# Two transformer blocks on one core: the first block's modulation as row dots beside the projections, norms beside the opening products, constants and gate rows made early

## The chip, the core and the metric

The kernel runs on one core of a Trainium2 chip. A core has TensorE (PE, matrix products into PSUM; the profile shows its weight loads as PEld), VectorE (DVE), ScalarE (ACT), GpSimd (POOL) and SyncE (SP, which here issues nearly all DMA transfers). The engines run side by side and wait for each other on semaphores. The metric is device time in microseconds, the median of the runs.

## The reference

Sequence 256, width 1024, everything in fp32. The first block takes `x` and a context `ctx` of 256 tokens; the second block has four layers. What the change touches of the first:

```python
mod_l = jax.nn.silu(c) @ ada_w[i] + ada_b[i]          # 6 x 1024 columns
mod_c = jax.nn.silu(c_ctx) @ ada_w[i] + ada_b[i]
hl = rmsnorm(xl, norm1_g[i]) * (1.0 + sc1) + sh1      # and hc from the context
yc, yl = token_mixing(hc, hl, w_in[i], w_out[i], ...) # recurrence, neighbour attention, short convolution
xl = xl + g1 * yl
hl2 = rmsnorm(xl, norm2_g[i]) * (1.0 + sc2) + sh2
xl = xl + g2 * peer_ffn(hl2, ...)                     # 16 of 16384 experts in each of 8 heads
return rmsnorm(xl, final_g)
```

In the second block each layer computes `mod = silu(c) @ ada_w[i] + ada_b[i]` with 9 x 1024 columns, and runs a feed-forward part, a mixer (a sparse attention with compressed keys, stick-breaking, differential, sparse again) and a second feed-forward part, each behind a norm that is scaled and shifted by `mod`.

## The kernel before

The program is a series of blocks. In a block each engine has its own instruction list; between two blocks all five engines meet. So an operation that stands alone in a block holds everybody.

Weights of the projections come as items of 1 MB through a ring of six slots (`issue_w`), weights of the modulation as items through a ring of four slots (`issue_a`, `a_ring`). SP issues an item when its slot has been used. A unit is sixteen products of 128x256, two halves with eight steps of the contraction each; the profile shows an fp32 product as two instructions.

The first block, in order:
- An input block loads seven tensors; ACT makes the Silu of both conditions (L3169 on).
- `ada_stage`: DVE adds `item * cond[k]` into two accumulators of 128x2048, for eight items and two conditions. The partition sum is still open.
- `mod1_columns_stage`: `mod_columns` closes it on PE, one product with a column of ones for every 128 columns of the accumulator, so 32 products with one moving column (L377).
- `norm_stage`, twice, for `x` and for the context: squares on ACT, root, scaling on DVE, 16 transposes on PE, gain and shift on ACT into `hT` and `hcT`.
- `first_projections`: 21 units on PE with `hT` and `hcT`. Beside them the side work of `loads` and `work`: SP issues up to four modulation items behind each weight item, DVE multiplies and adds them (L238) into `rest` and `acc`. These are the other 4 x 1024 columns of the first block's modulation and the 9 x 1024 of the second block's layer 0.
- `mod1_rest_stage`: 104 products with the column of ones, then bias, gain and shift.
- `neighbour_stage`: loads the relative bias of the eight heads (2 MB), masks it on POOL with four selects, makes the short convolution on DVE, then runs the attention.
- `recurrent_mixer`: loads seven constants and waits for them, then four tile stages, `rw_chain_stage` (two chains of eight states, forward and backward, a link each for PE and DVE in turn) and `rw_output_stage`, which loads `g_up`.
- `rows1_stage`: spreads four modulation rows over all partitions, 32 products with the identity (L2567). Then output projection, second norm, and `peer_stage`, in which POOL gathers the experts' rows and DVE and PE weigh them.
- `final_norm_stage` loads `final_g` and `mod_stage` spreads three gate rows (24 products, L409).

In the second block, `compress` loads two constants and waits; `diff_stage` has a block of its own between projections and attention, which loads two constants and makes one scalar of them; `second_block` opens with two tables that ACT loads and waits for.

The order of each engine's list is the order in which the functions are called; no planner moves anything.

Of the kernel before, what the change touches and what calls it, by code (L numbers as in the profile page):

```python
# [39 lines left out]
M_COLS = 2 * D  # L40
MIXERS = ("nsa", "stick", "diff", "nsa")
# [55 lines left out]
class Core:  # L97


    def __init__(self, nc, ctx):  # L100
        self.nc = nc
        self.ctx = ctx
        self.signals = {}
        self.serial = 0
# [14 lines left out]
    def semaphore_of(self, name):  # L119
        if name not in self.signals:  # L120
            self.signals[name] = Signal(self.ctx.enter_context(self.nc.semaphore(name)))
        return self.signals[name]

    def sb(self, ctx, name, shape, dtype=F32):
        self.serial += 1
        return ctx.enter_context(self.nc.sbuf_tensor(f"{name}_{self.serial}", shape, dtype))
# [74 lines left out]
    def issue_a(self, sp, take):  # L201

        for n in range(self.a_issued, self.a_issued + take):
            if n >= self.a_first + A_SLOTS:
                sp.wait_ge(self.a_used, n - A_SLOTS + 1)
            if n < MOD1_ITEMS:
                sp.dma_start(self.a_ring[:, n % A_SLOTS, 0:M_COLS], self.m_stream[n]).then_inc(
                    self.a_loaded[n % A_SLOTS], 16)
            else:
                sp.dma_start(self.a_ring[:, n % A_SLOTS, :], self.a_stream[n - MOD1_ITEMS]).then_inc(  # L210
                    self.a_loaded[n % A_SLOTS], 16)
# [10 lines left out]
    def load_a(self, sp, n, turn=0):  # L222

        sp.wait_ge(self.a_used, turn * A_SLOTS + (n - A_SLOTS + 1))
        src = self.a_stream[bass.ds(turn * A_SLOTS + (n - MOD1_ITEMS), 1), :, :]
# [3 lines left out]
    def mod_unit(self, dve, n, cond, acc, turn=0, opens=False):  # L229
# [4 lines left out]
        if opens:  # L234
            last = dve.tensor_scalar(acc, item, cond, None, ALU.mult)
        else:
            dve.wait_ge(self.a_used, turn * A_SLOTS + (n - 1))
            last = dve.scalar_tensor_tensor(out=acc, in0=item, scalar=cond, in1=acc, op0=ALU.mult, op1=ALU.add)  # L238
# [24 lines left out]
def norm_stage(core, post, pre, of=None):  # L263

    nc = core.nc
    squares, roots = core.semaphore_of("squares_ready"), core.semaphore_of("roots_ready")
    means, rows = core.semaphore_of("means_ready"), core.semaphore_of("rows_ready")
    turned, x_new = core.semaphore_of("turned_ready"), core.semaphore_of("x_new")  # L270

    x, hT, gain, shift = of or (core.x, None, core.gain, core.shift)
    whole_made = core.semaphore_of("h_whole_made")
    y = core.y
    n_post = 1 if post is not None else 0
    n_pre = 1 if pre is not None else 0
    with ExitStack() as ctx:
        junk = core.sb(ctx, "junk", [P, 2, D])
        ss = core.sb(ctx, "ss", [P, 2, 2 * TT])
        stat = core.sb(ctx, "stat", [P, 4, TT])  # L280
        xn = core.sb(ctx, "xn", [P, TT, D])

        whole = junk[:].rearrange("p t (k n) -> p (t k) n", n=T)
        block = ctx.enter_context(nc.Block())

        @block.sync
        def _(sp):
            core.issue_w(sp, 0)

        @block.scalar  # L290
        def _(act):
            if n_post:
                for i in range(2 * TT):

                    act.activation(junk[:, i // 2, (i % 2) * BANK:(i % 2 + 1) * BANK], y[:, i, :], ACT.Square,
                                   accum_out=ss[:, 0, i:i + 1]).then_inc(squares.sem, 1)
                act.wait_ge(means.sem, means.at(1))
                act.activation(stat[:, 0, :], stat[:, 0, :], ACT.Sqrt).then_inc(roots.sem, 1)
# [1697 lines left out]

# [1381 lines left out]
```

## Time and profile before

| | us |
|---|---|
| median of 3 runs | 3866.25 (3865.90 to 3875.92) |
| the profiled execution, its time / span | 3875.92 / 3875.5 |
| PE busy | 3151.6 (81% of the span) |
| DVE busy | 2452.2 (63%) |
| ACT busy | 1294.1 (33%) |
| POOL busy | 569.5 (15%) |
| DMA moved | 860.09 MB, mean 222 GB/s |

The shares are means over stages with different limits. An engine that is idle says something only together with what the others do in the same stretch, and PE's granted clock (1.00 is 2.4 GHz, 0.50 is 1.2 GHz) has to be read beside PE's busy time.

### The profile page before, as it was taken

How to read it: one execution, taken by the hardware profiler on the slowest of the kernel's cores; microseconds unless marked ns; L12 is line 12 of the kernel's file. 1: busy time of each engine (PE TensorE's matmuls, PEld its weight loads, DVE VectorE, ACT ScalarE, POOL GpSimd, SP SyncE). 2: the span in 40 equal slices, each digit the busy share in tenths (PEclk: the TensorE clock that was granted, in tenths of full speed). 3: DMA queues.
4: the chain of work that ended last, by engine and by line, in shares of the span. 5: the costliest groups of instructions: out<-in, count | busy, mean ns of one | idle time of the engine just before them, and what ended most of it. 6: DMA issues, size and time to landing. Idle time of an engine off the chain costs nothing. (4 is left out here: it accounts for less than half of the span.)

```text
span 3875.5 us, 53219 instructions
## 1 busy us (share of the span) xinstructions
PE 3151.6 (81%) x21732; PEld 2669.1 (69%) x21732; DVE 2452.2 (63%) x3818; ACT 1294.1 (33%) x2068; POOL 569.5 (15%) x310
## 2 busy tenths in 40 slices
PE   3965776566665659988999998899998899997899
PEld 3854665322221129987898996898997799987798
DVE  3654553788888867736586854686853686543654
ACT  1003321111111123436434345434344434342733
POOL 0001001344444520030000013000004000012000
PEclk9966787777766679987999997999998999996999
DMA  4971001899999968631585842484943484553143
GB/s 184 403 304 44 2 3 57 307 368 375 382 369 390 391 285 353 228 145 44 218 323 209 355 146 97 194 340 190 367 155 124 190 344 152 185 184 121 45 175 129
DMA packets 118255, 860.09 MB, mean 222 GB/s; under 512 B 15152, under 2 KB 16304, under 8 KB 17712
## 3 DMA queue, kind: packets, MB, share of 16 engines
q1 hardware_dynamic: 80912, 588.77, 39.4%
q0 software_dynamic: 36864, 268.45, 17.3%
q8 instruction: 127, 2.08, 0.2%
q14 instruction: 64, 0.52, 0.0%
q10 hardware_dynamic: 288, 0.26, 0.0%
HBM read 856.38 MB, written 1.05 MB: 221 GB/s over the span
## 5 line engine op out<-in xcount | busy, mean ns | idle before, releaser
L252 PE MATMUL ps<-h_hi,w_hi 128*128 128x256 f32 x3328 | 951.7, 286 | 38.4 <-DVE h_lo L533 16.0
L254 PE MATMUL ps<-h_hi,w_lo 128*128 128x256 f32 x3328 | 947.4, 285 | 0.0
L253 PE MATMUL ps<-h_lo,w_hi 128*128 128x256 f32 x3328 | 947.4, 285 | 0.0
L179 DVE TENSOR_TENSOR w_lo<-w_ring,w_hi 128x2048 fp32r<-128x2048 f32 x284 | 649.7, 2290 | 466.4 <-ACT w_hi L174 464.8
L174 ACT ACTIVATE w_hi<-w_ring 128x2048 fp32r<-128x2048 f32 x330 | 630.0, 1914 | 683.1 <-PE ps L254 556.6
L252 PEld LDWEIGHTS ps<-h_hi,w_hi 128*128 128x128 f32 x3328 | 640.7, 193 | 52.1 <-issue 22.0
L253 PEld LDWEIGHTS ps<-h_lo,w_hi 128*128 128x128 f32 x3328 | 640.5, 192 | 3.2
L254 PEld LDWEIGHTS ps<-h_hi,w_lo 128*128 128x128 f32 x3328 | 640.5, 192 | 0.0
L2958 PE MATMUL ps<-expert_rows,expert_diag 128*128 128x512 f32 x512 | 381.0, 889 | 290.3 <-ACT expert_diag L2996 290.1
L179 POOL TENSOR_TENSOR w_lo<-w_ring,w_hi 128x2048 fp32r<-128x2048 f32 x46 | 212.2, 4632 | 2276.4 <-ACT w_hi L174 2276.4
L2958 PEld LDWEIGHTS ps<-expert_rows,expert_diag 128*128 128x128 f32 x512 | 120.7, 259 | 544.6 <-ACT expert_diag L2996 442.6
L2920 POOL DMA_INDIRECT expert_rows<-in_experts,expert_idx x256 | 343.9, 1343 | 415.5 <-DVE expert_sum L3108 218.1
L238 DVE SCALAR_TENSOR_TENSOR mod_acc<-a_ring,cond,mod_acc 128x2304 f32<-128x2304 f32 (+1 forms) x138 | 353.6, 2588 | 52.9 <-DMA a_ring<-in_a_stream 25.4
L3094 DVE CUSTOM_DVE_ANT_0 expert_junk<-expert_rows,h 128x1024 f32<-128x1024 f32 x256 | 309.6, 1224 | 102.4 <-DMA expert_rows<-in_experts,expert_idx 102.2
L254 PE MATMUL ps<-w_hi,hid_lo 128*128 128x512 f32 x704 | 277.2, 394 | 0.0
L252 PE MATMUL ps<-w_hi,hid_hi 128*128 128x512 f32 x704 | 275.4, 391 | 0.0
L253 PE MATMUL ps<-w_lo,hid_hi 128*128 128x512 f32 x704 | 275.3, 391 | 0.0
L2981 ACT ACTIVATE expert_coef<-expert_dot 128x2 f32<-128x2 f32 x128 | 26.0, 203 | 488.6 <-DVE expert_dot L3094 488.5
L252 PE MATMUL ps<-w_hi,h_hi 128*128 128x256 f32 x544 | 159.5, 293 | 19.1 <-POOL w_lo L179 9.7
L3108 DVE SCALAR_TENSOR_TENSOR expert_sum<-expert_rows,expert_coef,expert_sum 128x1024 f32<-128x1024 f32 x128 | 164.5, 1285 | 4.5
L253 PE MATMUL ps<-w_lo,h_hi 128*128 128x256 f32 x544 | 158.2, 291 | 0.0
L254 PE MATMUL ps<-w_hi,h_lo 128*128 128x256 f32 x544 | 158.2, 291 | 0.0
(454 smaller groups left out, 4319.7 us busy)
## 6 DMA issues: line engine op xcount, KB each, us to landing
w_ring<-in_w_stream SPq DMA_DIRECT2D x360, 1024.0 KB, 4.9
a_ring<-in_a_stream SPq DMA_DIRECT2D x128, 1152.0 KB, 11.0
a_ring<-in_m_stream SPq DMA_DIRECT2D x24, 1024.0 KB, 9.7
mod_acc<-in_mod_start SPq DMA_DIRECT2D x6, 2304.0 KB, 8.8
alibi<-in_alibi SPq DMA_DIRECT2D x3, 2048.0 KB, 8.7
expert_rows<-in_experts,expert_idx POOLq DMA_INDIRECT x256, 9.2
a_ring<-in_norm_post_row SPq DMA_DIRECT2D x3, 1024.0 KB, 4.7
na_bias<-in_na_bias SPq DMA_DIRECT2D x1, 2048.0 KB, 8.0
```

What stands on the lines that cost most here:

```text
L174: act.activation(self.w_halves(n)[0], self.w_item(n), ACT.Copy).then_inc(self.hi_made, 1)
L179: pool.tensor_tensor(self.w_halves(n)[1], self.w_item(n), self.w_halves(n)[0], ALU.subtract).then_inc(self.lo_made, 1)
L238: last = dve.scalar_tensor_tensor(out=acc, in0=item, scalar=cond, in1=acc, op0=ALU.mult, op1=ALU.add)
L252: pe.matmul(out, stationary[0], moving[0], start=start, stop=False)
L253: pe.matmul(out, stationary[0], moving[1], start=False, stop=False)
L254: return pe.matmul(out, stationary[1], moving[0], start=False, stop=stop)
L2920: pool.indirect_dma_start(rows[:, slot, :], None, core.io["experts"], bass.IndirectOffsetOnAxis(ap=idx[:, n // UNIT, at:at + 1], axis=0)). ...
L2958: last = pe.matmul(core.y[:, 2 * t + half, :], diag[:, b % G_BATCHES, :], rows[:, n % G_SLOTS, D + half * BANK:D + (half + 1) * BANK], sta ...
L2981: act.activation(coef[:, b % G_BATCHES, :], dot[:, b % G_BATCHES, :], ACT.Gelu_apprx_tanh).then_inc(acts.sem, 1)
L3094: last = dve.tensor_tensor_reduce(junk[:, e, :], rows[:, slot, 0:D], core.h2[:, tile_of(n), :], 1.0, 0.0, ALU.mult, ALU.add, dot[:, b % G_ ...
L3108: dve.scalar_tensor_tensor(out=acc[:, t, :], in0=rows[:, n % G_SLOTS, D:2 * D], scalar=c[:, 0:1], in1=acc[:, t, :], op0=ALU.mult, op1=ALU. ...
```

## The change

1. **Opening.** `opening_stage` replaces five blocks. PE multiplies the conditions, as two stationary columns, with the items themselves, so that the sum over the partitions comes at once: 8 items x 4 banks, products of 2x512. The norms of `x` and the context run on DVE beside them, and PE's 32 transposes of them stand between the products of items 3 and 4 and between those of 6 and 7. Two rows of 2048 come out; 16 small transposes turn them into columns.
2. **Row dots.** The other modulation weights come transposed, 52 items of 1 MB with two groups of 128 output columns each. An output column's weights lie along a partition, so one `tensor_tensor_reduce` with the condition row gives the finished column (`mod_dots`); its elementwise output goes back into the item. `mod1_rest_stage` is gone.
3. **Constants early.** The neighbours' bias goes out first in the projections' block and POOL masks it there; the convolution moves to POOL beside the attention (`beside`); the recurrence's constants and `g_up` are loaded in the opening, `final_g` in `peer_stage`, the compression's and the differential attention's in the projections ahead. ACT's wait for two tables moves to DVE in the attention (`prepare`), and so does the scalar of the differential attention.
4. **Wide rows.** `rows1_stage` and `mod_stage` are gone; their 14 half rows are made inside `rw_chain_stage`, one behind each link (`widen`), with ACT's copies.
5. In the expert loop the dot's elementwise output goes back into the gathered row, and DVE no longer waits there for its own previous dots.

```diff
+    def mod_dots(self, dve, n, cond_row, cols):
+        dve.wait_ge(self.a_loaded[n % A_SLOTS], (n // A_SLOTS + 1) * 16)
+        for b in range(2):
+            rows = self.a_ring[:, n % A_SLOTS, b * D:(b + 1) * D]
+            last = dve.tensor_tensor_reduce(rows, rows, cond_row, 1.0, 0.0, ALU.mult, ALU.add, cols[:, b:b + 1])
+        last.then_inc(self.a_used, 1)
...
+        @block.tensor            # opening_stage
+            pe.wait_ge(cond_made.sem, cond_made.at(1))
+            for k in range(KD):
+                pe.wait_ge(core.a_loaded[k % A_SLOTS], (k // A_SLOTS + 1) * 16)
+                for c in range(M_COLS // BANK):
+                    last = pe.matmul(core.ps[0:2, c, :], cond[:, k, :],
+                                     core.a_ring[:, k % A_SLOTS, c * BANK:(c + 1) * BANK],
+                                     start=(k == 0), stop=(k == KD - 1))
+                last.then_inc(core.a_used, 1)
+                if k == 3:
+                    pe.wait_ge(ident_in.sem, ident_in.at(16))
+                    turns(0, xn)
+                if k == 6:
+                    turns(1, xc)
+            pe.wait_ge(rows_out.sem, rows_out.at(2))
+            for c in range(2 * KD):
+                last = pe.transpose(core.ps[:, 0, 2 * c:2 * c + 2], rows[:, c * P:(c + 1) * P], core.ident[0:2, 0:2])
...
+            def loads(sp, items):
+                sp.dma_start(a.na_bias[:], core.io["na_bias"]).then_inc(bias_in.sem, 16)
+                total = core.a_taken + T_ITEMS
+                for _ in range(items):
+                    core.issue_w(sp, 1)
+                    core.issue_a(sp, min(-(-T_ITEMS // items), total - core.a_taken))
...
+            def widen(i):        # rw_chain_stage
+                cols = halves[i][0]
+                if i >= 4:
+                    pe.wait_ge(wide_kept.sem, wide_kept.at(i - 3))
+                for j in range(4):
+                    last = pe.matmul(core.y[:, i % 4, j * P:(j + 1) * P], wide(cols[:, j], P), core.ident[:],
+                                     start=True, stop=True)
+                last.then_inc(wide_out.sem, 1)
...
-                if b:
-                    dve.wait_ge(dots.sem, dots.at(b))
...
-                    last = dve.tensor_tensor_reduce(junk[:, e, :], rows[:, slot, 0:D], ...
+                    last = dve.tensor_tensor_reduce(rows[:, slot, 0:D], rows[:, slot, 0:D], ...
```

Three places show how the lists change. PE's list in the opening, before (`mod_acc` are DVE's sums, `xn` the scaled tokens):

```order
L377 MATMUL ps<-ones,mod_acc 128x1 x32
L2485 UNCONDITIONAL_BRANCH
L353 UNCONDITIONAL_BRANCH [waits barrier_Pool_Activation_PE_DVE_SP_release]
L359 MATMUL ps<-identity,xn 128x128 [waits rows_ready]
L359 MATMUL ps<-identity,xn 128x128 x15
L277 UNCONDITIONAL_BRANCH
L353 UNCONDITIONAL_BRANCH [waits barrier_Pool_Activation_PE_DVE_SP_release]
L359 MATMUL ps<-identity,xn 128x128 [waits rows_ready]
L359 MATMUL ps<-identity,xn 128x128 x15
L277 UNCONDITIONAL_BRANCH
```

and after (`cond` are the two stationary columns; the tile `na_bias` lends its room to the scaled tokens and `na_v` to the two rows):

```order
L2465 MATMUL ps<-a_ring,cond_42 2x512 [waits a_loaded3]
L2465 MATMUL ps<-a_ring,cond_42 2x512 x3
L2456 MATMUL ps<-identity,na_bias 128x128 [waits open_scaled,ident_in]
L2456 MATMUL ps<-identity,na_bias 128x128 x15
L2465 MATMUL ps<-a_ring,cond_42 2x512 [waits a_loaded0]
L2465 MATMUL ps<-a_ring,cond_42 2x512 x3
L2465 MATMUL ps<-a_ring,cond_42 2x512 [waits a_loaded1]
L2465 MATMUL ps<-a_ring,cond_42 2x512 x3
L2465 MATMUL ps<-a_ring,cond_42 2x512 [waits a_loaded2]
L2465 MATMUL ps<-a_ring,cond_42 2x512 x3
L2456 MATMUL ps<-identity,na_bias 128x128 [waits open_kept,open_scaled]
L2456 MATMUL ps<-identity,na_bias 128x128 x3
```

The products follow the items one by one, and the norms' transposes stand among them; the five meetings of the engines in the first list are one. DVE's list beside the projections, before and after:

```order
L238 SCALAR_TENSOR_TENSOR mod_acc<-a_ring,cond_25,mod_acc 128x2048 [waits a_used,a_loaded2]
L238 SCALAR_TENSOR_TENSOR mod_acc<-a_ring,cond_25,mod_acc 128x2048 [waits a_used,a_loaded3]
L238 SCALAR_TENSOR_TENSOR mod_acc<-a_ring,cond_25,mod_acc 128x2048 [waits a_used,a_loaded0]
L238 SCALAR_TENSOR_TENSOR mod_acc<-a_ring,cond_25,mod_acc 128x2048 [waits a_used,a_loaded1]
L238 SCALAR_TENSOR_TENSOR mod_acc<-a_ring,cond_25,mod_acc 128x2048 [waits a_used,a_loaded2]
```

```order
L252 ISA a_ring,mod_cols_38<-a_ring,cond_rows 128x1024 [waits a_loaded0]
L252 ISA mod_cols_38 128x1
L252 ISA a_ring,mod_cols_38<-a_ring,cond_rows 128x1024
L252 ISA mod_cols_38 128x1
L252 ISA a_ring,mod_cols_38<-a_ring,cond_rows 128x1024 [waits a_loaded1]
```

A scalar multiply and add over 2048 or 2304 columns becomes two reductions of 1024, each followed by the read of its accumulator; the wait for the item before last (`a_used`) is gone. PE's list in the chain of states, before and after:

```order
L2349 MATMUL ps<-state,psi 64x64 x3
L2349 MATMUL ps<-state,psi 64x64 [waits state_kept1]
L2349 MATMUL ps<-state,psi 64x64 x3
L2349 MATMUL ps<-state,psi 64x64 [waits state_kept0]
L2349 MATMUL ps<-state,psi 64x64 x3
L2349 MATMUL ps<-state,psi 64x64 [waits state_kept1]
```

```order
L2225 MATMUL ps<-state,psi 64x64 x3
L2217 MATMUL ps<-identity,cols_15 128x128 [waits mod_wide_kept]
L2217 MATMUL ps<-identity,cols_15 128x128 x3
L2225 MATMUL ps<-state,psi 64x64 [waits state_kept1]
L2225 MATMUL ps<-state,psi 64x64 x3
L2217 MATMUL ps<-identity,cols_15 128x128 [waits mod_wide_kept]
L2217 MATMUL ps<-identity,cols_15 128x128 x3
L2225 MATMUL ps<-state,psi 64x64 [waits state_kept0]
```

Behind the four products of each link stand four wide ones, from the fifth group on with a wait for ACT's copy of four groups before.

## Rows read from the trace of the kernel before

**Rows 1.** Stretch, us; busy PE, PEld, DVE, ACT, POOL; PEclk, DMA share, GB/s.
```profile
93.30:264.00 170.70, 134.65 (x624) 118.56 (x622) 114.49 (x48) 12.33 (x21) 0.00 (x0) 0.90 0.98 406
228.00:264.00 36.00, 0.00 (x0) 0.00 (x0) 29.02 (x12) 0.58 (x1) 0.00 (x0) 0.54 0.99 414
264.20:309.00 44.80, 44.50 (x208) 44.45 (x208) 0.39 (x2) 0.00 (x0) 0.00 (x0) 0.50 0.01 3
695.00:1415.00 720.00, 424.13 (x718) 158.56 (x717) 595.80 (x1262) 92.14 (x285) 343.92 (x256) 0.73 0.94 377
1452.30:3875.50 2423.20, 2245.98 (x15856) 2082.61 (x15856) 1480.09 (x1958) 1056.91 (x1513) 193.91 (x42) 0.93 0.52 200
```

**Rows 2.** Timeline, opening and first projections: start, us, engine, operation.
```profile
17.79 31.76 DVE L917 SCALAR_TENSOR_TENSOR mod_acc<-a_ring,cond,mod_acc 128x2048 f32<-128x2048 f32 x14
...
80.59 3.75 ACT L308 ACTIVATE hcT<-ps,shift,gain 128x256 f32<-128x256 f32 x8 [2.86 <-PE ps L359]
...
84.63 8.63 PE L977 MATMUL ps<-w_ring,hT 128*128 128x256 f32 x32 [1.52 <-PEq L277]
106.92 7.07 PE L977 MATMUL ps<-w_ring,hcT 128*128 128x256 f32 x32
```

**Rows 3.** Stretches with 128x512 fp32 products alone, at either clock.
```profile
714.00:718.00 4.00, 3.78 (x4) 1.17 (x4) 4.00 (x11) 0.36 (x2) 1.68 (x1) 0.50 1.01 426
1409.10:1412.90 3.80, 3.70 (x8) 1.44 (x8) 2.23 (x4) 0.40 (x2) 0.00 (x0) 1.00 1.00 414
```

**Rows 4.** DMA issues of the first 100 us: size, median us to landing.
```profile
x<-in_x_in SPq DMA_DIRECT2D x1, 1024.0 KB, 4.9
```

**Rows 5.** Stretches with small PE instructions: the chain of states, the wide rows.
```profile
574.60:590.00 15.40, 14.61 (x134) 13.31 (x135) 12.52 (x30) 0.00 (x0) 0.00 (x0) 0.54 0.01 2
610.00:615.10 5.10, 5.05 (x46) 4.86 (x44) 1.52 (x4) 1.79 (x3) 0.00 (x0) 1.00 0.00 0
```

**Rows 6.** Page, part 5: two groups of one shape on ACT and POOL.
```profile
L174 ACT ACTIVATE w_hi<-w_ring 128x2048 fp32r<-128x2048 f32 x330 | 630.0, 1914 | 683.1 <-PE ps L254 556.6
L179 POOL TENSOR_TENSOR w_lo<-w_ring,w_hi 128x2048 fp32r<-128x2048 f32 x46 | 212.2, 4632 | 2276.4 <-ACT w_hi L174 2276.4
```

**Rows 7.** Timeline of DVE: last modulation item, and a reduction of 1024.
```profile
261.29 2.62 DVE L238 SCALAR_TENSOR_TENSOR mod_acc<-a_ring,cond,mod_acc 128x2304 f32<-128x2304 f32 x1 [0.18 <-DMA a_ring<-in_a_stream]
...
1418.53 1.23 DVE L3318 CUSTOM_DVE_ANT_0 final_junk<-x 128x1024 f32<-128x1024 f32 x1
```

**Rows 8.** Timeline around the neighbour attention: before it, its start, after it.
```profile
309.83 0.17 DVE L2548 SCALAR_TENSOR_TENSOR cols<-mod_sums,norm_g 128x8 f32<-128x8 f32 x1
...
334.82 2.08 PE L2641 MATMUL ps<-na_kT,na_qT 64*128 64x512 f32 x4 [26.09 <-PEq L2701]
...
378.65 0.42 DVE L2116 TENSOR_TENSOR kk<-k,rw_rows 128x256 f32<-128x256 f32 x1 [9.76 <-PEq L2752]
```

**Rows 9.** The masks' stretch, and DVE's 128x256 operation in and out of it.
```profile
318.00:332.50 14.50, 0.00 (x0) 0.00 (x0) 13.73 (x7) 0.00 (x0) 13.25 (x4) 0.50 0.00 0
...
322.36 11.44 DVE L2737 SCALAR_TENSOR_TENSOR sc_o<-sc_u,sc_w,sc_o 128x256 f32<-128x256 f32 x6
...
387.82 0.42 DVE L2132 SCALAR_TENSOR_TENSOR early<-early,rw_rows 128x256 f32<-128x256 f32 x1
```

**Rows 10.** Timeline: wide rows, final gain, gate rows, first products of two stages.
```profile
605.65 9.41 PE L2567 MATMUL ps<-identity,cols 128*128 128x128 f32 x64 [0.93 <-PEq L2394]
...
1426.86 2.48 DVE L3325 SCALAR_TENSOR_TENSOR x<-x,final_ss,final_g 128x1024 f32<-128x1024 f32 x2 [6.45 <-DMA final_g<-in_final_g]
...
1429.64 6.96 PE L409 MATMUL ps<-identity,gate_cols 128*128 128x128 f32 x48 [16.79 <-PEq L3299]
...
1440.90 7.17 PE L543 MATMUL ps<-ones_r 128*128 128x512 f32 x20 [4.30 <-PEq L1841]
...
2964.10 2.53 PE L1465 MATMUL ps<-kT,qT 64*128 64x128 f32 x12 [7.18 <-PEq L1759]
```

**Rows 11.** Tile cmp_blk: its engine sat idle until, us, times.
```profile
  DMA cmp_w<-in_cmp_w: 9.2, 2
```

More of the change, by code:

```diff
@@ L374, in mod_columns @@
-def mod_columns(core, pe, acc, chunks, bank):
-    for c in range(chunks):
-        last = pe.matmul(core.ps[:, bank, c:c + 1], acc[:, c * P:(c + 1) * P], core.ones[:, 0:1],
-                         start=True, stop=True)
-    return last
 def shape_columns(core, dve, layer, cols, subs):
@@ L1007, in _ @@
         def _(pool):
+            if side:
+                side[2](pool)
             for n in splits:
@@ L2333, in rw_chain_stage @@
     y_done = core.semaphore_of("rw_y_done")
+    wide_out, wide_kept = core.semaphore_of("mod_wide"), core.semaphore_of("mod_wide_kept")
+    wide_rows = [(m.cols[:, v, :], m.rows[:, v, :]) for v in range(4)]
+    wide_rows += [(core.gate_cols[:, sub, :], core.gates[:, sub, :]) for sub in range(3)]
+    halves = [(cols[:, 4 * half:4 * half + 4], row[:, half * BANK:(half + 1) * BANK])
+              for cols, row in wide_rows for half in range(2)]
     def part(d):
@@ L2468 @@
 PROJ1 = 14
-MOD1_FIRST = KD
 class Mod1:
@@ new lines, in constants @@
+            def constants(sp):
+                io = core.io
+                for dst, src in ((g[:], io["norm2_g"]), (core.norm_pre[:], io["norm_pre"]),
+                                 (core.norm_post[:], io["norm_post"]),
+                                 (bias[:, 0:REST_COLS], io["mod_bias1"][:, 2 * KD:]),
+                                 (bias[:, REST_COLS:], io["mod_bias2"][:, 0, 0, :])):
+                    sp.dma_start(dst, src).then_inc(late_consts.sem, 16)
+                sp.dma_start(a.sc_w[:], io["sc_w"]).then_inc(conv_in.sem, 16)
+                tables.load(core, sp)
@@ new lines, in work @@
+            def work(dve):
+                done = core.dve_steps.done
+                for i in range(T_ITEMS):
+                    row = cond_row[:, 0 if 2 * i < REST_COLS else 1, :]
+                    core.mod_dots(dve, MOD1_FIRST + i, row, cols[:, 2 * i:2 * i + 2])
+                dve.wait_ge(late_consts.sem, late_consts.at(80))
+                dve.wait_ge(core.a_used, A_BASE)
+                done(dve, dve.tensor_tensor(cols[:], cols[:], bias[:], ALU.add))
+                rest = cols[:, 0:REST_COLS].rearrange("p (v k) -> p v k", v=4)
+                by_sub = cols[:, REST_COLS:].rearrange("p (s a k) -> p s a k", s=3, a=3)
+                shape_columns(core, dve, 0, by_sub, range(3))
+                dve.tensor_tensor(core.gate_cols[:], by_sub[:, :, 2, :], core.norm_post[:], ALU.mult)
+                done(dve, dve.tensor_copy(m.cols[:], rest))
+                dve.scalar_tensor_tensor(out=m.cols[:, 2, :], in0=rest[:, 2, :], scalar=1.0, in1=g[:],
+                                         op0=ALU.add, op1=ALU.mult)
@@ L3227, in first_block @@
             short.close()
-            recurrent_mixer(core, a, outT)
-        m.rows = core.sb(ctx, "rows1", [P, 4, D])
-        rows1_stage(core, m)
+            m.rows = core.sb(ctx, "rows1", [P, 4, D], side="right")
+            recurrent_mixer(core, m, a, tables, outT)
         with ExitStack() as s0:
```

703 lines of the change are left out of this document (278 added, 425 removed).

## The prediction

> **What bounds the kernel now.** I read the busy time by stretches first, then the timeline of each stretch in which TensorE (PE) is idle, then the waits on DMA in the later stages. The stretches show four kinds of bound. From 93.3 to 264.0 us the DMA share is 0.98 at 406 GB/s: the weights of the projections and of the modulation go through one pipe, and in the last 36 us of it (228 to 264) PE does nothing at all while the DMA share is 0.99. From 264.2 to 309 us PE does 208 LDWEIGHTS-bound instructions with one moving column each, all others idle. From 695 to 1415 us the gather of the experts holds the DMA engines at 0.94. From 1452 to the end PE is busy 2246 of 2423 us at a clock of 0.93; no line of that work changes, apart from three waits [rows 1]. So the change can gain only in the serial places around these.
>
> The opening is serial: VectorE (DVE) sums eight items for two conditions until 49.55 us (17.79 + 31.76), PE adds up the columns, the two norms follow one after the other, and the projections begin at 84.63 us [rows 2].
>
> **Part 1, the opening.** Added: 32 products of 2 x 512 (eight items, four banks). An fp32 product shows as two instructions, so 64. A 128x512 instruction of the same kind took 3.78/4 = 0.945 us at clock 0.50 and 3.70/8 = 0.46 us at 1.00 [rows 3]; they have 128 stationary columns where the new ones have 2, but the moving 512 columns set the time. The input x landed 4.9 us after its issue [rows 4]; x is now issued at about 1.2 us and the first item right behind it, at 1 MB in 2.5 us (406 GB/s), so item 0 is there at about 8.6 us. PE starts at the low clock. At 84.63 us the first 32 instructions of the projections took 8.63 us where 32 later ones took 7.07 [rows 2], an excess of 1.6 us, so some 3.3 us at the low level; I take 4 of the 64 instructions at 0.945 us and 60 at 0.46 = 31.5 us. The 32 transposes of the norms lie between them on PE: 46 instructions of that width took 5.05 us at clock 1.00, 0.11 each [rows 5], so 3.5 us. PE is done at 8.6 + 31.5 + 3.5 = 43.6 us. DMA isn't the limit: ten pieces of 2.5 us land by about 29 us when the ring is free, and each item takes PE 3.7 us. The norm's squares and scaling on DVE (about 5 us each) end before PE reaches them. Behind PE's last product: a copy of 2 x 1024 (1.1 us and a hop of 0.25), 16 transposes of two rows (0.11 to 0.23 each, I take 1.8 us), DVE's sums, shift and gain (0.9), ACT's eight pieces (3.75, [rows 2]), a table load and the two Silu, the wide one of the shape that takes ACT 1.91 us [rows 6], with the load 3.4 us together, and 0.3 us to the next stage (84.34 to 84.63 in [rows 2]). Sum 55.1 us, against 84.6: **gain 29.5**. Bounds: all 64 at the low clock is 64 x 0.945 = 60.5 us in place of 31.5, gain 0.5; with all at 0.46 it is gain 31.5.
>
> **Part 2, dots beside the projections.** The side work was 16 items of 1 MB and 32 of 1.125 MB, 52 MB; it is now 52 items of 1 MB, again 52 MB. The stretch stays bound by DMA where it was (0.98 of 170.7 us, [rows 1]), so it keeps its length: 179.3 us from PE's start to the last sum (84.6 to 263.9). DVE per item: two dots of 1024. Such a reduction took 1.23 us [rows 7], so with the hop 2.5 us for 1 MB, against 2.62 us for 1.125 MB. That is 52 x 2.5 = 131 us of 179: not the bound, though inside a burst of four items it is level with DMA's 2.5 us. The 2 MB of the neighbours' bias go out ahead of the rest, in the 8.7 us in which the queue waits for PE's first unit anyway: 0. The dots end at 55.1 + 179.3 = 234.4 us. I bound this by -3 (a shorter last item) and +8.
>
> **Part 3, what followed them.** Gone: the 208 column sums, the load of the bias and its masks, the convolution on DVE. Between the last item (261.29 + 2.62 = 263.91, [rows 7]) and the first score product (334.82, [rows 8]) lay 70.9 us. What is left of it on DVE is a dozen operations of 0.17 us in a chain (row of 309.83, [rows 8]), 1.2 us, and the change of stage, 0.3: **gain 69.4**. The masks now run on GpSimd (POOL) beside the first dots, the convolution on POOL beside the attention: four two-input operations of 512 at 4632/2048 = 2.26 ns a column [rows 6] are 4.6 us, six of 256 some 3.5, with memset and waits 10 us, below the 34 us of that stage (334.82 to 378.65 less 9.76, [rows 8]). Hidden, but not free: while POOL's masks ran, DVE's 128x256 operation took 11.44/6 = 1.9 us and without them 0.42 [rows 9], 4.5 times as long. Beside the attention this can touch ten microseconds of DVE work of which one operation in a dozen is of that kind: between 0 and +8, I take **-3**. Beside the dots, masks (13.3 us [rows 9] from the landing of the bias at about 8 us after PE's start) and dots (from 16 us after it) overlap some 6 us: DVE loses 4.5 us and has 3.3 us of slack in each of the first bursts, which come two units of 6.9 us apart (7.07 with its overlap, [rows 2]): 0 in the sum, +4.5 as the bound.
> The Trainium skill, page GPSIMD Engine Reference, section 8 Key points, says that GpSimd shares its SBUF interfaces with VectorE and that Vector instructions with two SBUF inputs contend; every dot is one. By that rule the trace's factor holds for the dots too, and the sum is up to 4.5 us smaller.
>
> **Part 4, smaller waits.** The recurrence's constants come early: its first DVE operation sat idle 9.76 us [rows 8]; left are ACT's tanh and the change of stage, 0.65: **gain 9.1**. The rows of the second modulation: PE 9.41 us plus 0.93 us of edge go [rows 10], and 14 groups of four products (112 instructions) go into the chain of states. That chain takes some 15 us for seven pairs of links, 2.1 us each, on PE at clock 0.54, 134 instructions in 14.6 us or 0.11 each [rows 5]. The new instructions cost 112 x 0.11 = 12 us at the full clock and twice that at the low one. A pair of links then holds twice eight link instructions (0.44 us at the full clock) and twice eight new ones (0.88), 2.6 us instead of 2.1: +3.8 for seven pairs, +2 until the clock rises, and -2 for the 64 output instructions behind it, which find the clock up; PE becomes the engine that is late: +4. At the low clock (0.88 + 1.76) x 2 = 5.3 us per pair: +22. DVE waits for the link products, and nobody but PE's own queue stands behind a group; ACT's 14 copies of 512 columns, some 0.5 us each by the rate of [rows 6], fit. **Gain 10.3 - 4 = 6.3**, down to -12. The later gate rows go whole: 6.96 us and an edge of 1.0: **8.0**. The final gain row: DVE's 6.45 us wait, **6.4**. ACT's wait for two tables is inside PE's 4.30 us gap at 1440.9; its issues stay: **2.0**, between 0 and 4. The compression's constants: **9.2** in two waits [rows 11]. The differential attention's separate stage: PE idle 7.18 us, of which the issue-free rest is kept: **5.2** [rows 10]. The dropped wait in the expert loop and the in-place output gain 0, since the gather holds that stage at 0.94 of DMA [rows 1]; one broadcast of 0.5 MB ahead of it costs at most 1.3 us, which I leave in the range.
>
> **The sum.** 29.5 + 69.4 - 3 + 9.1 + 6.3 + 8.0 + 6.4 + 2.0 + 9.2 + 5.2 = 142.1 us. The profiled execution took 3875.92 us, so it would take 3733.8; the median of the runs is 9.7 us below it, so 3866.25 - 142.1 = **3724 us**.
>
> **The rivals.**
> *The opening stays at the low clock.* The granted clock stayed at 0.50 through 44.8 us in which PE was busy 44.5 of them with one-column products [rows 1], and at 0.54 in the chain of 64x64 ones [rows 5]: being busy isn't enough. For the rise: 128x512 instructions did run at 1.00 [rows 3], and the new ones stream as many columns. Time 3724 + 29 = 3753.
> *The chain of states stays at the low clock.* 3724 + 18 = 3742. For it: 0.54 there now; against it: the same products as a block got 1.00 from 610 us on [rows 5].
> *POOL slows DVE more than the slack covers.* At the upper bounds, 4.5 + (8 - 3) = 9.5: 3734.
> *The dots become the bound, slower than before.* If a dot in place took much longer than 1.26 us, the stretch would be 52 items long on DVE. Place: the projections. It overtakes DMA from 179.3/52 = 3.4 us per item, and eats the whole gain at (170.7 + 142)/52 = 6.0 us per item, 3.0 us per dot; at 3.3 us per dot the kernel would take 3866 + 31 = 3897. Against it: the in-place sum of 2304 columns took 2.62 us, 1.14 ns a column [rows 7], and the reduction out of place takes 1.23 for 1024, 1.20 ns; only POOL's factor of 4.5 would reach it, and POOL works 13 of those 171 us.
> *Nothing is won,* because the stage is bound by DMA alone: against it, DMA idles in nearly all of the removed places.
>
> **How the numbers follow.** Forecast 0.62 (own range 3710 to 3738); opening at the low clock 0.17; chain at the low clock 0.12; POOL 0.06; dots the bound 0.02; nothing won 0.01. The range reaches down to the better bounds (-18: clock, last item, waits) and up to the first rival: 3706 to 3756. This kernel's measurement tells 0.3%, 12 us, from no change. Faster 0.97, same 0.01, slower 0.02.
>
> **What would show it.** Projections begin at about 55 us (84 if the first rival holds), with PE's granted clock 1.00 over most of 12 to 43 us. First neighbour scores at about 236 us. From there to the recurrence's first DVE operation 35 to 37 us, without the 9.8 us gap. The chain of states 19 to 20 us long. From 264 us on no one-column products. The forecast is wrong if the dots take over 1.7 us each, if PE waits for items in the opening, or if the clock of the second block isn't within 0.01 of 0.93.

## The result, and the profile after

The changed kernel takes 3762.20 us (median of 4 runs, 3761.18 to 3767.77), the kernel before 3871.09 us (4 runs, three of them those under "Time and profile before"; 3865.90 to 3883.90). The ratio is 0.9715, 95% interval 0.9696 to 0.9734: faster. The forecast was 3724 us, range 3706 to 3756. The direction was right, the size wasn't: the change was to save 142 us, and the two spans differ by 3875.5 - 3760.8 = 114.7 us.

Long stretches of the kernel after (stretch, us; busy PE, PEld, DVE, ACT, POOL; PEclk, DMA share, GB/s). They answer to [rows 1] and, in the chain of states, to [rows 5]:

```profile
12.00:43.00 31.00, 31.00 (x93) 8.39 (x91) 4.13 (x8) 2.15 (x5) 0.00 (x0) 1.00 0.99 387
...
62.50:236.40 173.90, 135.25 (x627) 118.72 (x625) 127.83 (x208) 12.33 (x21) 13.29 (x4) 0.90 0.98 399
...
473.50:515.40 41.90, 41.87 (x224) 37.13 (x224) 12.21 (x29) 7.76 (x13) 0.00 (x0) 0.51 0.00 1
515.40:520.00 4.60, 4.52 (x65) 4.33 (x64) 0.69 (x1) 0.60 (x1) 0.00 (x0) 0.50 0.00 0
585.20:1326.20 741.00, 444.03 (x832) 177.47 (x832) 610.39 (x1328) 94.45 (x288) 341.61 (x256) 0.74 0.93 371
1347.00:3760.80 2413.80, 2248.99 (x15856) 2084.97 (x15856) 1480.67 (x1958) 1056.73 (x1513) 193.94 (x42) 0.93 0.53 201
```

From 12 to 43 us the opening shows a granted clock of 1.00, DMA bounds the projections as before, and the second block has its 0.93. The third row is the surprise: in the chain of states PE is busy 41.87 of 41.90 us, at 0.51, the low one of its two levels (1.2 GHz).

The timeline after, first PE and DVE from the opening to the neighbour attention (start, us, engine, operation), for [rows 2, 7 and 8]:

```profile
9.12 16.17 PE L2465 MATMUL ps<-a_ring,cond 128*2 128x512 f32 x32 [9.12 <-DMA a_ring<-in_m_stream]
...
27.12 10.46 PE L2465 MATMUL ps<-a_ring,cond 128*2 128x512 f32 x24
...
39.41 3.59 PE L2465 MATMUL ps<-a_ring,cond 128*2 128x512 f32 x8
...
53.79 9.28 PE L802 MATMUL ps<-w_ring,hT 128*128 128x256 f32 x32 [8.34 <-PEq L2365]
...
73.04 4.25 DVE L252 CUSTOM_DVE_ANT_0 a_ring<-a_ring,cond_rows 128x1024 f32<-128x1024 f32 x1
...
235.11 1.22 DVE L252 CUSTOM_DVE_ANT_0 a_ring<-a_ring,cond_rows 128x1024 f32<-128x1024 f32 x1
...
237.98 2.93 PE L2561 MATMUL ps<-na_kT,na_qT 64*128 64x512 f32 x6 [40.23 <-PEq L768]
...
274.20 0.42 DVE L1972 TENSOR_TENSOR kk<-k,rw_rows 128x256 f32<-128x256 f32 x1 [0.55 <-PEq L2642]
```

and then the chain of states, the norm, and the first products of the second block and of the differential attention, for [rows 10]:

```profile
475.80 1.11 PE L2225 MATMUL ps<-state,psi 64*64 64x64 f32 x8
...
476.84 2.07 PE L2217 MATMUL ps<-identity,cols 128*128 128x128 f32 x8
...
1331.21 2.48 DVE L3198 SCALAR_TENSOR_TENSOR x<-x,final_ss,final_g 128x1024 f32<-128x1024 f32 x2
1335.59 7.50 PE L399 MATMUL ps<-ones_r 128*128 128x512 f32 x20 [11.97 <-PEq L1680]
...
2847.13 0.93 PE L1326 MATMUL ps<-kT,qT 64*128 64x128 f32 x8 [1.71 <-PEq L768]
```

The wait for `final_g` is gone, the differential attention's 7.18 us are 1.71. A link with its wide group takes 1.04 + 2.00 = 3.04 us (from 475.80 to 476.84, and to the next link at 478.84), and there are fourteen.

Lining both timelines up at the same operations says where the time went. The prediction's terms stand in the last column; a negative gain is time lost.

| from, to | before, us | after, us | gain | forecast |
|---|---|---|---|---|
| start to first projection | 84.63 | 53.79 | 30.8 | 29.5 |
| to the end of the last modulation sum | 179.3 | 182.5 | -3.3 | 0 |
| to the first neighbour score | 70.9 | 1.7 | 69.3 | 69.4 |
| to the recurrence's first DVE operation | 43.8 | 36.2 | 7.6 | 6.1 |
| four tile stages | 196.4 | 199.3 | -2.9 | 0 |
| chain, outputs, rows, to the output projection's first product | 49.7 | 67.6 | **-17.9** | **+6.3** |
| output projection, norm, to the expert stage | 44.5 | 44.0 | 0.5 | 0 |
| expert stage, to the last update of x | 746.3 | 741.0 | 5.2 | 0 |
| to the second block's first product | 25.4 | 9.4 | 16.1 | 16.4 |
| second block | 2434.6 | 2425.2 | 9.4 | 14.4 |

Up to the recurrence 104.4 us are gained where 105.0 were forecast. One line alone is far off, by 24.2 us.

### The profile page after: what moved, and what is told of

Read it like the earlier page. It is cut to its first block and busy times, and to the rows that moved or that the text cites. A ratio compares the mean times of both kernels' runs of the same rounds, so it can differ in the third digit from the quotient of the medians.

```text
span 3760.8 us, 52720 instructions
## 1 busy us (share of the span) xinstructions
PE 3137.1 (83%) x21540; PEld 2628.7 (70%) x21540; DVE 2418.7 (64%) x3961; ACT 1296.3 (34%) x2066; POOL 580.9 (15%) x321
## 3 DMA queue, kind: packets, MB, share of 16 engines
q0 software_dynamic: 36864, 268.45, 17.9%
q8 instruction: 125, 2.05, 0.2%
## 5 line engine op out<-in xcount | busy, mean ns | idle before, releaser
L266 PE MATMUL ps<-h_hi,w_hi 128*128 128x256 f32 x3328 | 951.0, 286 | 39.5 <-DVE h_lo L389 16.1
L2971 DVE CUSTOM_DVE_ANT_0 expert_rows<-expert_rows,h 128x1024 f32<-128x1024 f32 x256 | 309.1, 1223 | 100.7 <-DMA expert_rows<-in_experts,expert_idx 100.6
L244 DVE SCALAR_TENSOR_TENSOR mod_acc<-a_ring,cond,mod_acc 128x2304 f32<-128x2304 f32 x96 | 247.3, 2613 | 14.6 <-issue 14.1
L252 DVE CUSTOM_DVE_ANT_0 a_ring<-a_ring,cond_rows 128x1024 f32<-128x1024 f32 x104 | 127.5, 1264 | 58.6 <-DMA a_ring<-in_t_stream 55.1
```

The source lines that it names most:

```text
L252: last = dve.tensor_tensor_reduce(rows, rows, cond_row, 1.0, 0.0, ALU.mult, ALU.add, cols[:, b:b + 1])
L266: pe.matmul(out, stationary[0], moving[0], start=start, stop=False)
L2971: last = dve.tensor_tensor_reduce(rows[:, slot, 0:D], rows[:, slot, 0:D], core.h2[:, tile_of(n), :], 1.0, 0.0, ALU.mult, ALU.add, dot[:, b ...
```

## The experiments

**No wide products, or all behind, ahead, or hidden.** The theory: the wide products are paid at the low clock in the chain because of what they stand among. The rivals: they cost that anywhere here, or the chain waits for something else.

wide_none takes the groups out, and ScalarE copies its rows from `x`, so the wide rows are left out of the computation:

```diff
-                    widen(2 * (n - 1) + d)
...
-                act.wait_ge(wide_out.sem, wide_out.at(i + 1))
-                act.activation(row, core.y[:, i % 4, :], ACT.Copy).then_inc(wide_kept.sem, 1)
+                act.activation(row, core.x[:, 0, 0:BANK], ACT.Copy).then_inc(wide_kept.sem, 1)
```

wide_behind puts them behind the last link, wide_ahead the same loop ahead of the first:

```diff
-                    widen(2 * (n - 1) + d)
+            for i in range(len(halves)):
+                widen(i)
```

wide_gaps makes them in three later stages (`make` is `widen` with the bank as an argument):

```diff
+            w.make(pe, 0, core.y[:, 0, :])
             pe.wait_ge(gate.sem, gate.at(1))
...
+            for i in (1, 2):
+                w.make(pe, i, core.y[:, i, :])
             pe.wait_ge(done.sem, done.at(1))
...
+                for i in range(3, 7):
+                    w.make(pe, i, core.ps[:, i - 3, :])
...
+            for i in range(7, 14):
+                m.wide.make(pe, i, core.ps[:, i % 4, :], i - 3 if i > 10 else 0)
             pe.wait_ge(rows.sem, rows.at(TT))
```

> The changed kernel without the 56 wide products in the chain of states (112 instructions): ScalarE fills the four modulation rows and the three gate rows from x instead, so the modulation rows and gates are left out of the computation. Theory A (the wide products hold the chain at TensorE's low clock and PE is what is late): the 14 links shrink from 41.9 us to the 13.8 us that they took in the kernel before (575.05 to 588.89), the rest stays: 3762 - 28 = 3734 us. Rival B (the chain waits for something else too, ScalarE's copies or the semaphores of the groups): the links take clearly more than 14 us, say 20, and the time is 3740 or more. Second question: with no other change the second block's length may still differ by some us from 2425.2, as its clock rises at other moments.

> The same 14 wide groups, but as one block behind the last link, ahead of the output products. Theory A (it is the 64x64 link products between them that keep the clock at 0.50; a block of 128x128 products raises it): links 13.8 us, block 9.41 us for 64 instructions as in the kernel before plus 48 more at 0.11 = 14.7 us, outputs at the full clock 2.3 us: 30.8 us in place of 41.9 + 4.5 = 46.4, so 3762 - 15.6 = 3746 us, with the granted clock at 1.00 in the last ten us of the block. Rival B (the wide products cost 0.26 us each wherever they stand in this stage): 13.8 + 29 + 4.5 = 47.3 us, time 3763 us and a clock of 0.50.

> The same 14 wide groups as one block ahead of the first link, at the start of the chain's stage. Theory A: the block takes 14.7 us with the clock rising in it; the links then start at the full clock and keep it as long as their 64x64 products allow. If the clock stays up, the links take 10 to 11 us instead of 13.8 and the outputs 2.3: 27.5 us in place of 46.4, time 3743 us; if it falls back within the first links, 13.5 + 4.5 us: 32.7 us, time 3748 us. Rival B (0.26 us per wide instruction wherever they stand here): 3763 us.

> The same wide groups moved into places where TensorE idles behind the chain: one ahead of the output gates' products and two behind them (gaps of 3.1 and 5.4 us), four at the head of the output projection (gap of 9.5 us, PE waits for the split weights), seven beside the gated sum and norm (gap of 13.4 us). Theory A: 28.1 us go from the chain; even at 2.07 us a group the first seven fit their gaps, the last seven (14.5 us at the low clock, 7.3 us at the full one) overrun by 1 us at most: 3762 - 28 + 1 = 3735 us. Rival C (what is hidden on PE comes back on ScalarE: its copies stand ahead of the splits and of the root): the output projection or the norm starts 3 to 6 us later, 3740 us. Rival D (PE busy in the gaps has the clock up when the projection starts): 5 us less, 3730 us.

Measured, with the kernel before at 3878.43 us in this batch (9 runs): wide_none 3732.14 us (ratio 0.9625, 0.9611 to 0.9639), wide_behind 3745.82 (0.9658, 0.9643 to 0.9673), wide_ahead 3744.27 (0.9662, 0.9645 to 0.9679), wide_gaps 3732.80 (0.9626, 0.9609 to 0.9642).

The timeline of PE with the block behind the links:

```profile
485.19 9.30 PE L2217 MATMUL ps<-identity,cols 128*128 128x128 f32 x64
494.32 5.52 PE L2217 MATMUL ps<-identity,gate_cols 128*128 128x128 f32 x48
499.78 2.69 PE L2235 MATMUL ps<-state,rw_qT 64*64 64x64 f32 x64
```

The stretches of the kernel with the block ahead: the block's beginning and end, then the links:

```profile
472.50:476.90 4.40, 4.34 (x26) 4.37 (x27) 0.84 (x2) 1.19 (x2) 0.00 (x0) 0.65 0.00 0
477.00:486.80 9.80, 9.80 (x88) 9.74 (x86) 0.00 (x0) 6.47 (x11) 0.00 (x0) 0.99 0.01 2
486.80:489.00 2.20, 1.53 (x26) 1.33 (x24) 1.33 (x4) 0.60 (x1) 0.00 (x0) 1.00 0.00 0
489.00:491.00 2.00, 1.52 (x19) 1.10 (x17) 1.87 (x5) 0.00 (x0) 0.00 (x0) 0.97 0.00 0
491.00:493.00 2.00, 1.77 (x16) 1.78 (x16) 1.60 (x5) 0.00 (x0) 0.00 (x0) 0.50 0.00 0
```

The rival of a fixed price is out: as a block the 112 instructions take 14.6 us in place of 28, and the last 48 take 5.52 us, 0.115 each, less than half of the 0.26 in the chain. Behind the block the outputs take 2.69 us instead of 4.52. Ahead of the links the block has the clock at 1.00, and the links alone lose it again: it is at 0.50 some 4 us after their start. Without wide products the links took 13.5 us, as in the kernel before: nothing else hung on them. Nor is it the chance of one execution: in the five other traces whose chain has the groups in this form (again, expert_wait, no_masks, no_bias and late_consts, all below) it took 41.9 to 42.3 us, at 0.51 each time. Hidden in pauses of PE they cost nothing that shows (3732.80 against 3732.14 without any): wide_gaps already beats both kernels.

**Each group twice.** I had by then a strict form of the theory: the 64x64 products between the groups hold the clock down.

```diff
-                for j in range(4):
+                for j in (0, 1, 2, 3, 0, 1, 2, 3):
```

> The changed kernel with each wide group in the chain made twice (sixteen instructions of 128x128 behind each link's eight of 64x64, in place of eight; the result is the same). Theory A in its strict form (the link products between the groups hold the clock at 0.50 whatever the share of the wide ones): 14 x 2.07 = 29 us more, 71 us for the chain, time 3791 us. Rival L (it is the share of wide products that counts, and 16 to 8 is enough for the clock to rise): the chain ends at 14 x (0.6 + 2 x 1.04) = 38 us with the clock at 1.00, less than the 41.9 us of the single groups, time 3758 us.

Measured: 3761.54 us (4 runs; the kernel before 3879.20; ratio 0.9690, 0.9674 to 0.9707). That time can't be told from the changed kernel's; the trace can. The timeline of PE and the stretch of the chain:

```profile
470.36 3.51 PE L2217 MATMUL ps<-identity,cols 128*128 128x128 f32 x16
473.80 0.80 PE L2225 MATMUL ps<-state,psi 64*64 64x64 f32 x8
474.53 2.05 PE L2217 MATMUL ps<-identity,cols 128*128 128x128 f32 x16
476.51 0.67 PE L2225 MATMUL ps<-state,psi 64*64 64x64 f32 x8
```
```profile
469.70:507.50 37.80, 37.75 (x336) 35.05 (x336) 12.21 (x29) 7.76 (x13) 0.00 (x0) 0.95 0.00 1
```

The strict form falls: with twice the wide products the chain is 4.1 us shorter, sixteen wide instructions take 2.05 us where eight took 2.07, and the clock is 0.95 in the mean. PE was busy all the time in both kernels. So here the clock didn't go by PE's busy time as the profile counts it; with more wide work between the same links it was higher. What it goes by these runs don't tell.

**The groups in the tile stages' pauses.** In the kernels so far the first half of a recurrence tile ran mostly at 0.50, with pauses of 2.64, 3.93 and 1.78 us on PE.

```diff
+WIDE_IN_TILE = ((0, 1, 2, 3), (4, 5, 6, 7), (8, 9, 10), (11, 12, 13))
+            made(pe, own[0])
             for d in range(2):
                 pe.wait_ge(s["wa_out"].sem, s["wa_out"].at(d + 1))
...
+            for i in own[1:-1]:
+                made(pe, i)
             pe.wait_ge(s["p_ready"].sem, s["p_ready"].at(2))
...
+            pe.wait_ge(s["turn1_out"].sem, s["turn1_out"].at(n_ch))
+            made(pe, own[-1])
```

> The changed kernel with its 14 wide groups taken out of the chain of states and set into PE's pauses in the four tile stages ahead of it (4, 4, 3, 3 groups: ahead of the decay sums' products, a pause of 2.64 us; ahead of the transposes, 3.93 us, one or two; behind the triangles, 1.78 us). All are hidden if they take no more than 2.07 us each; 28.1 us go from the chain as in the runs with no or hidden groups. Theory M (the wide products in the pauses raise the clock in the first half of a tile, in which PE now does some 15 us of work at 0.50): up to 5 us a tile less, 3762 - 28 - 20 = 3714 us. Rival N (the clock stays at 0.50 there, and the groups overrun their pauses by about 1 us a tile): 3762 - 28 + 4 = 3738 us.

> The same with each wide group in the tile stages made twice (16 instructions instead of 8; same result). Theory M: the clock rises earlier than with single groups, and a double group then takes 2.05 us, within its pause: as fast as the single groups or faster, 3710 us. Rival N: at 0.50 a double group takes 3.5 us, and the three or four pauses of a tile (2.64, 3.93 and 1.78 us) are overrun by 5 to 6 us: 3734 + 22 = 3756 us.

Measured, with the kernel before at 3878.19 us: wide_tiles 3729.21 us (5 runs, 3723.21 to 3734.46; ratio 0.9620, 0.9601 to 0.9638), wide_tiles2 3721.34 us (5 runs, 3718.96 to 3730.32; ratio 0.9600, 0.9584 to 0.9616). The second tile, 4 to 16 us from its start, in wide_gaps (no groups in the tiles), wide_tiles and wide_tiles2:

```profile
325.90:329.90 4.00, 4.00 (x21) 3.13 (x21) 0.12 (x1) 2.47 (x6) 0.00 (x0) 0.50 0.00 0
329.90:333.90 4.00, 1.71 (x4) 0.80 (x3) 3.42 (x9) 1.10 (x4) 0.00 (x0) 0.50 0.00 2
333.90:337.90 4.00, 2.37 (x11) 2.40 (x12) 1.39 (x4) 0.99 (x2) 0.00 (x0) 0.50 0.00 0
```
```profile
321.30:325.30 4.00, 4.00 (x25) 3.23 (x24) 0.81 (x3) 3.01 (x7) 0.00 (x0) 0.73 0.00 0
325.30:329.30 4.00, 2.51 (x17) 2.31 (x15) 3.76 (x10) 2.30 (x6) 0.00 (x0) 0.84 0.01 2
329.30:333.30 4.00, 2.91 (x24) 2.54 (x28) 0.26 (x1) 1.79 (x3) 0.00 (x0) 0.58 0.00 0
```
```profile
321.20:325.20 4.00, 4.00 (x34) 3.48 (x33) 0.82 (x3) 3.87 (x9) 0.00 (x0) 1.00 0.02 4
325.20:329.20 4.00, 2.67 (x24) 2.48 (x23) 3.76 (x10) 1.43 (x5) 0.00 (x0) 1.00 0.01 2
329.20:333.20 4.00, 2.82 (x78) 2.54 (x79) 0.30 (x2) 1.57 (x3) 0.00 (x0) 1.00 0.00 0
```

Theory M holds in kind: the four tiles take 192.5 and 189.3 us, against 196.4 to 199.9 in the kernels without groups there, so 4 to 7 and 7 to 11 us less in place of the 20 expected. Over the first 24 us of a tile the mean granted clock was 0.50 to 0.64 in the kernel before and the changed one, 0.60 to 0.79 in wide_tiles and 0.86 to 1.00 in wide_tiles2. So the doubled groups, which only repeat a result, had the clock up more, and wide_tiles2 has the lowest median of this study. That it is faster than wide_tiles isn't shown: the 8 us lie within the intervals, and its tiles' 3.2 us rest on one trace each, where kernels with the same tile code differ by 3.5 us.

**The expert stage and the size of chance.** The table shows 5.2 us in the expert stage that I hadn't forecast.

expert_wait is the changed kernel with the wait back; before_inplace is the kernel before with part 5 alone, that is without the wait and with the output in place; again is the changed kernel itself.

```diff
+                if b:
+                    dve.wait_ge(dots.sem, dots.at(b))
```
```diff
-                if b:
-                    dve.wait_ge(dots.sem, dots.at(b))
...
-                    last = dve.tensor_tensor_reduce(junk[:, e, :], rows[:, slot, 0:D], ...
+                    last = dve.tensor_tensor_reduce(rows[:, slot, 0:D], rows[:, slot, 0:D], ...
```

> The changed kernel itself once more, unchanged: a second profiled execution and more times, to see how far stages of the same code differ between executions. So far the expert stage (first query product to the last update of x) took 739 to 745 us in five kernels that have the same code there, and the second block 2421 to 2430 us. Theory E (these are differences between executions): here too it takes some value in 739 to 746 and 2420 to 2431, with no tie to the one seen before (741.1 and 2425.2). Rival F (they are set by the kernel, by when it reaches the stage): within 1 us of 741.1 and 2425.2. Time 3762 us, or up to 3770 in a batch in which the kernel before takes 3878.

> The kernel before with part 5 of the change alone: the dot's elementwise output goes back into the gathered row and VectorE doesn't wait for its previous dots. The expert stage was 746.3 us in the kernel before and 741.1 in the changed one, 5.2 us that my sum didn't have. Theory E (the stage is bound by the gather and differs between executions): a ratio of 1.000 to the kernel before, stage anywhere in 739 to 747 us. Rival G (the edit is worth 5 us): ratio 0.9987, stage 741.

> The changed kernel with the wait for the previous dots put back in the expert loop (the output stays in the gathered row). Theory E: same time as the changed kernel, 3762 us, stage in 739 to 746. Rival G in its other form (it is the wait that cost 5 us before): stage 746 us or more, 3767 us.

Measured, with the kernel before at 3876.50 us (16 runs): again 3760.97 us (0.9705, 0.9684 to 0.9726), before_inplace 3880.04 us (12 runs; 1.0009, 1.0000 to 1.0019), expert_wait 3762.64 us (0.9698, 0.9677 to 0.9720). Their expert stages took 738.6, 741.9 and 742.9 us. Part 5 of the change is worth nothing that these runs resolve, as forecast. Over all traces the expert stage lay between 734.4 and 748.1 us, the changed second block between 2420.6 and 2430.6. The stage in wide_tiles2, one of the longest, and in late_consts (below), the shortest:

```profile
544.40:1291.50 747.10, 442.57 (x832) 178.65 (x832) 610.34 (x1328) 94.45 (x288) 340.02 (x256) 0.75 0.93 368
```
```profile
593.10:1327.40 734.30, 439.14 (x832) 175.15 (x832) 610.72 (x1328) 94.44 (x288) 337.75 (x256) 0.74 0.94 374
```

The same instructions, DVE's busy time within 0.4 us, 368 against 374 GB/s (late_consts has one load of 0.5 MB less there). Terms of 5 us in these two stages can't be read from one trace of each kernel.

**The projections' 3.3 us.** Beside the selects the first two dots take 2.57 and 4.25 us instead of 1.22. Is that loss what lengthens the stretch?

no_masks leaves out the selects, no_bias the load as well:

```diff
-                mask_neighbours(core, pool, a.na_bias, bias_in)
+                pool.wait_ge(bias_in.sem, bias_in.at(16))
```
```diff
-                sp.dma_start(a.na_bias[:], core.io["na_bias"]).then_inc(bias_in.sem, 16)
+                sp.dma_start(a.na_bias[:, 0, 0, 0:16], core.io["na_bias"][:, 0, 0, 0:16]).then_inc(bias_in.sem, 16)
...
+                pool.memset(a.na_bias[:], 0.0)
```

> The changed kernel without the four selects that mask the neighbours' bias (so the mask is left out of the computation; the load of the bias stays). In the changed kernel the dots beside the selects took 2.57 to 4.25 us instead of 1.22, and from PE's first projection to the last dot it took 182.6 us where 179.3 were forecast. Theory H (VectorE's loss beside POOL's selects is what makes the stretch longer): without them 179.3 us, 3.3 us less, 3759 us. Rival I (the stretch is bound by DMA, and the 3.3 us are the 2 MB of the bias ahead of the other items, 5 us at 406 GB/s less some slack): the dots all take 1.22 us, the stretch stays at 182.6 us and the time at 3762 us.

> The changed kernel without the load of the neighbours' bias and without its mask: 8 KB are loaded in place of 2 MB, and POOL fills the tile with zeros (bias and mask are left out of the computation). Theory I (the 2 MB ahead of the first items lengthen the DMA-bound stretch): from PE's first projection to the last dot 179.3 us or less in place of 182.6, down to 177.6 if all 5 us of the load go; time 3762 - 4 = 3758 us. Rival K (the stretch is longer for its first bursts or its smaller items, not for the bias): 182 us again.

Measured: no_masks 3767.13 us (4 runs; ratio 0.9721, 0.9702 to 0.9741), no_bias 3763.06 us (4 runs; ratio 0.9694, 0.9676 to 0.9711); neither time can be told from the changed kernel's. All dots of no_masks, minimum, median and maximum in ns:

```profile
L252 DVE CUSTOM_DVE_ANT_0 a_ring<-a_ring,cond_rows x104: 1217/1223/1227, 69.4 to 234.2; 128x1024 f32<-128x1024 f32 x104
```

The dots are all at 1.22 us, and from the first projection (53.12) to the last dot's end it is still 182.3 us: the lost VectorE time was covered, as rival I says. Without the bias it is 181.0 us (53.78 to 234.81), 1.3 us less. But the same code took 181.5 to 184.0 us in the other traces, and the kernel before, 179.3 us in the trace of [rows 1], took 181.2 us in before_inplace (84.44 to 265.63), where nothing of this stretch is changed. So up to 1.9 of the 3.3 us are within what executions of one code differ by, and a share of the load isn't shown.

**Constants late again.**

```diff
+                tables.load(core, sp)
                 sp.wait_ge(consts.sem, consts.at(RW_CONSTS))
...
+            sp.dma_start(g[:], core.io["final_g"].partition_broadcast(P)).then_inc(loaded.sem, 16)
...
+            sp.dma_start(pe_col[:], core.io["cmp_pe"][j]).then_inc(consts.sem, 16)
+            sp.dma_start(w2[:], core.io["cmp_w2"][j]).then_inc(consts.sem, 16)
```

> The changed kernel with three groups of constants loaded late again, as in the kernel before: the recurrence's eight tables (the output gates' among them) at the start of the mixer, the final gain in the final norm, the compression's two tables in the compression. Theory A (the terms of my sum hold): the wait before the recurrence's first VectorE operation comes back with 9.1 us, the final gain's with 6.4, the compression's with 9.2 in two places: 24.7 us more, 3762 + 25 = 3787 us, ratio to the kernel before about 0.977. Rival J (part of it is covered by other work now, as stages are shorter): less than 20 us.

Measured: 3783.87 us (5 runs; ratio 0.9755, 0.9741 to 0.9768), 21.7 us above the changed kernel's first median. The waits, in timeline rows and the group of `cmp_blk`:

```profile
282.33 0.43 DVE L1973 TENSOR_TENSOR kk<-k,rw_rows 128x256 f32<-128x256 f32 x1 [8.88 <-PEq L2643]
```
```profile
1338.08 2.48 DVE L3199 SCALAR_TENSOR_TENSOR x<-x,final_ss,final_g 128x1024 f32<-128x1024 f32 x2 [5.71 <-DMA final_g<-in_final_g]
```
```profile
  DMA cmp_w<-in_cmp_w: 7.9, 2
```

(8.88 - 0.55) + 5.71 + 7.9 = 21.9 us, against 24.7 forecast, and the medians agree. The three waits are back, each 9 to 14% smaller than forecast. The profiled execution itself is the fastest of the five, 3770.28 us: its expert stage is 6.7 us shorter than the changed kernel's, and its second block takes 2426.3 us against 2425.2, so the compression's 7.9 us are seen as waits but not in the length of that block.

## Why the prediction was wrong

**The step that failed is the chain of states in part 4.** I wrote that the new instructions cost 0.11 us each at the full clock, allowed 2 us "until the clock rises", and so took +4 us for the chain and a gain of 6.3 us for the whole step. The price came from [rows 5], 610 to 615 us: a stretch of 128x128 products alone, at clock 1.00. The stretch into which they went was the other row of the same group, 0.54, and my first rival said of that very row that "being busy isn't enough"; I didn't apply it to the chain's own term. The runs put this in its place: 0.26 us per instruction (2.07/8), 28.4 us more for the links (13.5 to 41.9), no gain in the outputs (4.52 us in both kernels). Less the rows' stage, which did go, that is -17.9 in place of +6.3: 24.2 us of the 38.

**My rival had the right mechanism and too small a chance.** "The chain of states stays at the low clock" stood at 0.12 with 3742 us. I set against it that "the same products as a block got 1.00 from 610 us on": that they rise as a block is true (wide_behind), but they don't stand as a block there. Its size was short too: I took 5.3 us per pair of links at the low clock, it is 6.1, since the 128x128 instructions cost 0.26 us and not 2 x 0.11, and the link's eight 1.04 us and not 0.88; and the pair before was 13.5/7 = 1.9 us and not 2.1. Even that bound, +22, was 6 us short, and the range, whose upper end came from the first rival (3753), stopped 6 us below the time.

The Trainium skill, page TensorE: Matmul & The Clock Gate, section "Why this matters for your kernels", advises to keep TensorE continuously busy to get the full clock. The trace disagrees here: 41.87 of 41.90 us busy at 0.51. Interleaved work that merely closed PE's gaps wasn't enough; the measured runs decide.

**The rest of the 38 us.** 9.3 us come from the base: I subtracted the 9.7 us between the profiled execution and the median of three runs, and in the changed kernel that difference is 0.4 us (3762.57 against 3762.20). The kernel before came out at 3876.5 to 3879.2 us in four later batches, so 3866.25 was a low draw. Another 1.3 us lie between times and spans, and the other rows of the table come to 3.2 us less than forecast. Of them the tiles' -2.9, the expert stage's +5.2 and the second block's -5.0 lie inside the differences between executions that the runs show.

**What was right.** The opening: the 64 instructions of the eight items, with two stationary columns, took 30.2 us (16.17 + 10.46 + 3.59) where 31.5 stood. The first 32 took 0.505 us each in the mean, as the first six came about 0.85 us apart; the next 24 took 0.436 (10.46/24). PE was done at 43.0 us where 43.6 stood, and the projections began at 53.8 (55.1); the first rival is out. Part 2: dots of 1.22 us but for the two beside the selects, DMA the bound. Part 3: 69.3 of 69.4 us, and of the 9.2 us of wait that went at the recurrence 7.6 were gained, so the convolution on POOL cost the attention at most about 1.6 us where I took 3 (no run isolates it). The waits: 16.1 of 16.4 us between the experts and the second block; in the second block the compression's waits went, and the differential attention begins 7.18 - 1.71 = 5.5 us sooner (5.2).

## What to carry over

Price an instruction by a row in the state into which it goes, not by the cleanest row of its kind: on TensorE the granted clock of the receiving stretch is part of the price, and a stretch that is full of PE work can still be at the low level. Put side work into PE's pauses, where it cost nothing measurable here and came with a higher clock behind it, rather than behind links of a chain in which it makes PE the late engine. Before a time is forecast from one execution, ask how far the median of a few runs is itself a draw.

## What the runs showed of the hardware

- In the chain PE, busy 41.87 of 41.90 us, stayed at 0.51 with eight 128x128 instructions per eight 64x64 ones (0.51 in five further traces too), and had 0.95 with sixteen (one trace, wide_twice); the doubled work was 4.1 us shorter.
- 128x128 instructions alone had 0.65 in the first 4.4 us of their block and 0.99 in the next 9.8 (wide_ahead). The 64x64 links behind them, with PE busy 3.05 of 4.2 us, began at 1.00 and were then at 0.50.
- 128x128 products in PE's pauses made the four recurrence tiles shorter: 192.5 us with single groups and 189.3 with doubled ones, against 196.4 to 199.9 without (one trace of each kernel).
- Beside POOL's selects two DVE reductions of 128x1024 with two SBUF inputs took 2.57 and 4.25 us instead of 1.22; without the selects (no_masks) all 104 took 1.22 or 1.23.
- At clock 1.00 a 128x512 fp32 instruction took about as long with 2 stationary columns (0.45 us, 3.59/8) as with 128 (0.46, [rows 3]).
